# Moving the even K tiles' rows of two split operands inside their SBUF blocks

## The reference

```
h = concat(meta, x)
h = h + mixer(rmsnorm(h))            # w_in 2048 x 6152, attention and short convolution, w_out 2048 x 2048
h = h + (silu(h' @ w_gate) * (h' @ w_up)) @ w_down        # width 5632
x = rmsnorm(h)[16:]
h = x @ w_in_2                       # 2048 x 8192: q, k, v, u and two gates
merged = sig(gate_a) * (attn @ w_ba) + sig(gate_p) * (pool @ w_bp)
x = layer_norm(2**0.25 * x + merged @ w_out_2)
x = layer_norm(2**0.25 * x + relu(x @ w_ff1)**2 @ w_ff2)  # width 8192
```

## Time and profile before

| what | value |
|---|---|
| median of 3 runs | 2472.88 us |
| the profiled execution, its own time | 2471.54 us |
| its span, first to last instruction | 2469.7 us |
| TensorE matmul busy | 2439.0 us (99%) |
| TensorE weight load busy | 2172.6 us (88%) |
| VectorE busy | 1619.7 us (66%) |
| ScalarE busy | 1200.2 us (49%) |
| HBM read | 445.12 MB, 181 GB/s over the span |
| granted TensorE clock, mean | 0.997 |

### The profile page before, as it was taken

How to read it: one execution, slowest core, us unless ns; L and a number is a source line. 1 busy time by engine, 2 the same in 40 slices (tenths; PEclk the granted TensorE clock), 3 DMA queues, 4 the chain that set the end, 5 groups by cost and what they waited for, 6 DMA issues and landing times.

```text
span 2469.7 us, 36384 instructions
## 1 busy us (share of the span) xinstructions
PE 2439.0 (99%) x14746; PEld 2172.6 (88%) x14746; DVE 1619.7 (66%) x2471; ACT 1200.2 (49%) x1729; POOL 214.7 (9%) x231
## 2 busy tenths in 40 slices
PE   8999999999999999999999999999999999999996
PEld 8898898888888888888888888888998888888886
DVE  5645676766666665667677756678785665565667
ACT  6444545544444443445555654544454443443544
POOL 0001111000000000002221112023200000000022
PEclk9999999999999999999999999999999999999998
DMA  7554456566666566665655456565466656666663
GB/s 247 179 155 127 129 171 189 190 189 185 196 188 192 183 196 190 191 187 190 196 185 169 167 181 195 186 191 178 151 198 190 191 188 189 192 190 191 183 195 103
DMA packets 125752, 449.60 MB, mean 182 GB/s; under 512 B 13840, under 2 KB 16400, under 8 KB 125584
## 3 DMA queue, kind: packets, MB, share of 16 engines
q1 hardware_dynamic: 125296, 446.91, 57.8%
q10 hardware_dynamic: 288, 0.36, 0.0%
HBM read 445.12 MB, written 2.10 MB: 181 GB/s over the span
## 4 chain that ended last, share of the span: by engine, by line
PE 96%; DVE 3%; ACT 1%; issue 0%; DMA 0%; ACTq 0%; POOL 0%; POOLq 0%; DVEq 0%
PE out_bank L599 27%; PE out_bank L603 27%; PE out_bank L600 14%; PE out_bank L602 14%; PE out_bank L606 3%; PE out_bank L607 3%; PE out_bank L608 3%; DVE w_lo L1224 1%; PE side_bank L678 0%; ACT w_hi L833 0%; PE side_bank L677 0%; PE side_bank L716 0%; DVE h L1600 0%; DVE b_op L1655 0%; PE side_bank L707 0%
## 5 line engine op out<-in xcount | busy, mean ns | idle before, releaser
L1224 DVE TENSOR_TENSOR w_lo<-raw,w_hi 128x1024 fp32r<-128x1024 f32 x839 | 1040.4, 1243 | 603.5 <-ACT w_hi L833 599.4
L833 ACT CAST w_hi<-raw 128x1024 fp32r<-128x1024 f32 x840 | 877.9, 1049 | 959.1 <-PE out_bank L603 876.1
L599 PE MATMUL out_bank<-a_op,w_hi 128*128 128x512 f32 x1984 | 784.6, 395 | 1.4 <-DVE h L1251 0.8
L603 PE MATMUL out_bank<-a_op,w_hi 128*128 128x512 f32 x1984 | 776.7, 391 | 0.0
L600 PE MATMUL out_bank<-a_op,w_lo 128*128 128x256 f32 x1984 | 558.9, 282 | 0.0
L602 PE MATMUL out_bank<-a_op,w_lo 128*128 128x256 f32 x1984 | 552.1, 278 | 0.0
L602 PEld LDWEIGHTS out_bank<-a_op,w_lo 128*128 128x128 f32 x1984 | 380.1, 192 | 84.4
L600 PEld LDWEIGHTS out_bank<-a_op,w_lo 128*128 128x128 f32 x1984 | 372.9, 188 | 76.9
L599 PE MATMUL out_bank<-b_op,w_hi 128*128 128x512 f32 x992 | 389.8, 393 | 0.0
L603 PE MATMUL out_bank<-b_op,w_hi 128*128 128x512 f32 x992 | 388.0, 391 | 0.0
L599 PEld LDWEIGHTS out_bank<-a_op,w_hi 128*128 128x128 f32 x1984 | 373.1, 188 | 4.2 <-DVE w_lo L1224 1.8
(11 more groups left out here) (285 smaller groups left out, 2006.3 us busy)
## 6 DMA issues: line engine op xcount, KB each, us to landing
raw<-in_w_ff SPq DMA_DIRECT2D x256, 512.0 KB, 4.3
raw<-in_w_in SPq DMA_DIRECT2D x223, 512.0 KB, 3.7
raw<-in_w_gu SPq DMA_DIRECT2D x176, 512.0 KB, 4.2
raw<-in_w_down SPq DMA_DIRECT2D x88, 512.0 KB, 4.2
raw<-in_w_out SPq DMA_DIRECT2D x64, 512.0 KB, 4.3
raw<-in_w_ba SPq DMA_DIRECT2D x16, 512.0 KB, 3.8
raw<-in_w_bp SPq DMA_DIRECT2D x16, 512.0 KB, 4.1
out<-h SPq DMA_DIRECT2D x8, 256.0 KB, 2.1
```

The lines of the kernel that those rows point to most:

```text
L599: t_.e.matmul(bank[:, :], wh, a_both, start=start, stop=False, skip_group_check=True)
L603: mm = t_.e.matmul(bank[:, :], wh, a_both, start=False, stop=stop, skip_group_check=True)
L833: a.e.copy(w_hi[:, m % SPLIT, :], raw[:, u % RAW, :]).then_inc(hi_split)
L1224: v_.e.tensor_tensor(w_lo[:, m % SPLIT, :], raw[:, u % RAW, :], w_hi[:, m % SPLIT, :].bitcast(F32), ALU.subtract).then_inc(lo_split)
```

## The change

`PLACE` goes; a table `ROWS_AT` gives the first number of the hi and the lo row for even and odd K tiles, for each operand. The odd K tiles' rows stay at 564 and 822. The even ones go to 16 and 288 in `a_late` (64 and 1152 bytes, or 64 and 128 within 256), and to 0 and 258 in `b_op` (0 and 1032 bytes, or 0 and 8 within 256). The two-row access of L599 on `a_late` has a distance of 272 numbers between its rows in place of 258. Everything else, instructions, order and waits, is as before.

```diff
-        ROW, PLACE = SEQ + 2, 48
+        ROW = SEQ + 2
+
+        ROWS_AT = {"a": ((16, 288), (564, 822)), "b": ((0, 258), (564, 822))}
...
+        def rows_at(op, kt):
+            return ROWS_AT["b" if op is b_op else "a"][kt % 2]
+
         def part(op, kt, i, n=SEQ):
 
-            at = PLACE + ROW * (2 * (kt % 2) + i)
+            at = rows_at(op, kt)[i]
             return op[:, kt // 2, at:at + n]
 
         def parts(op, kt, n=SEQ):
-            at = PLACE + ROW * 2 * (kt % 2)
-            return op[:, kt // 2, at:at + 2 * ROW].rearrange("p (i t) -> p i t", i=2)[:, :, 0:n]
+            hi, lo = rows_at(op, kt)
+            return op[:, kt // 2, hi:hi + 2 * (lo - hi)].rearrange("p (i t) -> p i t", i=2)[:, :, 0:n]
 
         def affine_column(i, x):
-            rows = b_op[:, :, PLACE:PLACE + 4 * ROW].rearrange("p m (o i t) -> p m o i t", o=2, i=2)
-            return rows[:, :, :, i, SEQ + x]
+            even, odd = ROWS_AT["b"][0][i] + SEQ + x, ROWS_AT["b"][1][i] + SEQ + x
+            return b_op[:, :, even:odd + 1:odd - even]
```

## The result

The kernel after takes 2495.98 us (median of 4 runs, 2494.73 to 2497.66) against 2473.14 us: a ratio of 1.0093, interval 1.0077 to 1.0109. It is 22.8 us slower. I had forecast 2460.5 us, with 2446 to 2486 as the range.

A forecast was written before the change was run, and what follows sets the result against it. TensorE streaming its matmuls was taken to bound the kernel. The profiled 2471.54 us less 12.4 on the first operand, nothing for the second or the affine stage, gave 2459.1; as a median 2460.5 us, range 2446 to 2486.

The forecast's parts named there:

- What bounds the kernel, and that only the step of a group could move: TensorE streams matmuls for 96% of 2469.7 us; addresses could touch only 53 ns of a group's 693.3.
- Steps come in levels of 6.67 ns: Long stretches show only levels; groups on `a_late` drop one, 693.3 to 686.7 ns, 12.4 us less over 1856 groups.
- If each half brings its own time: On `a_late`, q's even half (665 ns) joined to gu1's odd half (669) gives a 684 ns group, 9 less.
- wrong at its root: Stated failure condition: the time of a half depends on the other half's places, so q's even half says nothing.
- The slower rival: Late stages on `a_late` take q's slow rhythm, 700.0 ns a group, 12.4 us more, 2485.3 us; chance 0.23.
- no change, since it is those finer places that stay: Groups on `b_op` keep 693.3 ns because places within 64 bytes stay; bound 6.6 us either way over 992 groups.
- The affine stage, at most 1.4 us less: 128 pairs of K tiles in three-matmul form could gain up to 1.4 us; nothing was taken.
- The rule of 16-byte lines: Each crossing to a new 16-byte line costs something: first operand would gain, second would not; no price given.
- The gap of N/2.4 + 2.5 ns: Isolated warm matmul's gap without addresses: 650 ns a group before and after, supporting no difference (2472.9 us, chance 0.27).

The follow-up runs named there:

- a_only: Only the first operand's even rows moved (64 and 128 within 256 bytes), the second operand left as in the kernel before: 2484.09 us, ratio 1.0045.
- b_only: Only the second operand's even rows moved (0 and 8 within 256 bytes), the first operand left as in the kernel before: 2486.25 us, ratio 1.0053.
- level686: Against the kernel before, both operands' rows at numbers 260, 814, 528, 0, odd pair read lo first, affine columns written apart: 2453.78 us, ratio 0.9924.
- level720: All four rows of both operands moved by 16 bytes against the kernel before (numbers 52, 310, 568, 826): 2511.25 us, ratio 1.0156.

## Why the prediction was wrong

*What bounds the kernel, and that only the step of a group could move:* right. Idle time, instruction counts and the side work are as before.

*Steps come in levels of 6.67 ns:* right in the long late stretches, where each operand before and after has a whole number of them (104, 105 and 106), and with it a_only, b_only and level686 were forecast within 1.5 us. As a law it is too strict. Other layouts settle at 690.0, 703.3 or 710.0; in several of them single groups differ and only a cycle of a few groups is a whole number.

*"If each half brings its own time":* this is the step that failed. I took the even half of q's group as if it stood by itself, 665 ns of records, and put it to the odd half of gu1, 669. After the change the even half has 397 + 277 = 674 and the odd one 397 + 279 = 676. Each is slower than it was in the stretch that I took it from, the odd one with rows that had not moved. Matmuls follow each other through one rhythm that all four rows and four weight tiles make, so a half carries its duration to no other group. I had written this down as what would make the prediction wrong at its root. The slower rival had 700.0 ns for the first operand, as measured, though it read that step off q, whose odd rows stand elsewhere. Its price, 12.4 us, came to 11.1 in a_only and to 10.7 in the lengths of the stages; beside the side matmuls some of the 1856 groups were above 693.3 before as well.

*The second operand, "no change, since it is those finer places that stay":* wrong, and the larger of the two errors. The place within 64 bytes doesn't decide; two levels were lost, 706.7 ns, and with 13.2 us b_only costs twice the bound of 6.6 that I had put on it. I had set that bound at one level with no row for it.

*The affine stage, at most 1.4 us less:* it shrank by 0.4 us, within the bound. In its steady part a pair of K tiles fell from 723 to 717 ns (40 of them take 28.67 us), so the sign was right; but the slow stretch behind its wait can hide that, as b_only shows with 1.2 us more for the same rows.

*The range* reached to the slow rhythm on the first operand alone (2486); the second operand's two levels put the time 10 us above it.

*The rule of 16-byte lines* (the Trainium skill, "SBUF — State Buffer", section "Specifications (TRN2)") would have let the first operand gain and the second stay. The runs go against both: the first operand's lo row now starts on a line and its groups take 700.0 ns against 693.3, and the second, with lines crossed as before, 706.7. *The gap of N/2.4 + 2.5 ns*, which the Trainium skill gives for an isolated matmul ("TensorE: Matmul & The Clock Gate", section "Back-to-back issue gap"), would make 650 ns for every layout; the layouts run took 686.7 to 726.7.

What stays open is what happens beneath. That rows and weight tiles count by their place against each other, with a pattern of 256 bytes, is shown for the layouts tried. That TensorE's reads of the rows and of the next weight tile meet in the same part of SBUF and one waits would fit, but it is a guess that no run shows, and I can't work out a layout's step from its places; it has to be measured.

## What to carry to other kernels

Where TensorE streams matmuls without a wait, look at the start-to-start step and not at the busy time; if it stands above the columns over the clock, the places of moving rows against weight tiles within 256 bytes are worth a search, here 5% between the slowest and the fastest layout that fit the block. Don't carry the duration of a matmul from one stretch to another whose neighbours read from other places: take a whole period of the exact sequence, or measure it. A kernel of nothing but that sequence measures a hundred layouts in 2 ms, and its steps came back in the long stretches of the whole kernel to 0.1 ns, provided that both rhythms of a layout are looked for; which of them the whole kernel takes it doesn't tell.

## What the runs showed that I had not expected

- The step of one 256-column matmul with its weight load ranges from 113.3 to 130.0 ns by the place of its row alone.
- A layout can have two steady rhythms: 720.0 and 706.7 ns for the one that level720 uses, 706.7 and 710.0 for the second operand's. Even within an unchanged stage this shows: q before had stretches at 693.3 and at 700.0, and after, with not one of its addresses changed, 18 groups from the middle of q (74.24 to 86.72 us) ran at 693.3.
- The traffic of VectorE, ScalarE and the DMA engines isn't needed for it: with all of it left out the same steps appear. Whether such traffic, or the side matmuls, pick between two rhythms is open.
- The affine stage's length changed by up to 2 us through something other than places, by the time that TensorE spends at the lower clock level after a wait of 3.4 us.
